# Hybrid decoder layer: prompt transposes first, two weight slots ahead of K, tile 3 ahead of the first page weights, memory tiles and last V pages one place sooner

## The reference, cut to what matters

```
h = x + W_out[ RMSNorm(stick_breaking(q, k, v)) | RMSNorm(B * conv3(C * xv)) ]     # q,k,v,B,C,xv = RMSNorm(x) @ W_in
h = h + cross_attention(RMSNorm(h), mk, mv)       # prompt: mk, mv = RMSNorm(mem) @ W_ck, @ W_cv
y = RMSNorm(h + SwiGLU(RMSNorm(h)))

def sb_block(z, mask, v, carry):
    log_om = where(mask, log_sigmoid(-z), 0)
    suffix = reverse_cumsum(log_om) - log_om + carry
    a = where(mask, exp(log_sigmoid(z) + suffix), 0)
    return a @ v, carry + sum(log_om)
```

## Time and profile before

| What | us |
|---|---|
| median of 3 runs | 1191.43 |
| their range | 1190.54 to 1193.67 |
| the profiled execution's own time | 1196.76 |
| its span (first to last instruction) | 1195.0 |
| TensorE busy in it | 1066.1 (89%) |
| VectorE, ScalarE, GpSimd busy | 665.4, 320.7, 409.5 |

### The profile page before, as it was taken

How to read it: one execution, slowest core, us unless ns; L and a number is a source line. 1 busy time by engine, 2 the same in 40 slices (tenths; PEclk the granted TensorE clock), 3 DMA queues, 4 the chain that set the end, 5 groups by cost and what they waited for, 6 DMA issues and landing times.

```text
span 1195.0 us, 28991 instructions
## 1 busy us (share of the span) xinstructions
PE 1066.1 (89%) x11527; PEld 913.7 (76%) x11527; DVE 665.4 (56%) x909; ACT 320.7 (27%) x486; POOL 409.5 (34%) x341
## 2 busy tenths in 40 slices
PE   5987999999678879787699889899999999999997
PEld 3765887866435545555599759899999999999996
DVE  2834566758478778563588348655543013544543
ACT  3511112222233524232423252412111112112121
POOL 0515354443323334344333013334333333433330
PEclk9988999999889889998799999899999999999999
DMA  9959687878999999784561132232222222231222
GB/s 352 333 167 328 203 296 245 285 268 273 392 337 329 326 325 318 277 325 146 194 227 37 40 118 91 71 106 70 82 76 72 87 94 82 72 103 44 67 66 80
DMA packets 126501, 221.16 MB, mean 185 GB/s; under 512 B 9951, under 2 KB 68580, under 8 KB 126388
## 3 DMA queue, kind: packets, MB, share of 16 engines
q1 hardware_dynamic: 103234, 146.63, 36.5%
q0 software_dynamic: 20480, 67.13, 15.9%
q10 hardware_dynamic: 2674, 5.87, 1.3%
HBM read 213.78 MB, written 5.80 MB: 184 GB/s over the span
## 4 chain that ended last, share of the span: by engine, by line
PE 66%; DVE 12%; DMA 8%; issue 5%; SPq 4%; ACT 2%; POOL 1%; POOLq 1%; DVEq 0%; ACTq 0%
PE ps L523 38%; PE ps L1664 11%; PE ps L1767 7%; DMA k_set<-in_cache_sb_k 4%; DMA mw_raw<-in_w_in 3%; DVE k_set L1342 2%; PE ps L1818 2%; SPq L618 2%; PE ps L584 2%; SPq L619 2%; DVE r_sq L699 2%; DVE r_sum L704 1%; DVE om_s L1361 1%; PE ps L367 1%; DVE h_lo L428 1%
## 5 line engine op out<-in xcount | busy, mean ns | idle before, releaser
L479 POOL TENSOR_TENSOR w_lo<-w_raw,w_hi 128x2048 fp32r<-128x2048 f32 (+3 forms) x49 | 192.9, 3939 | 404.2 <-ACT w_hi L456 363.6
L523 PE MATMUL ps<-h_hi,w_hi 128*128 128x288 f32 x832 | 180.5, 299 | 8.7 <-DVE h_lo L428 5.7
L523 PE MATMUL ps<-h_lo,w_hi 128*128 128x288 f32 x832 | 179.5, 298 | 0.0
L523 PE MATMUL ps<-h_hi,w_lo 128*128 128x288 f32 x832 | 179.5, 297 | 0.0
L1767 PE MATMUL ps<-k_set,q_blk 32*32 32x256 f32 x4096 | 135.2, 405 | 37.9 <-DVE k_set L1342 19.1
L1342 DVE STREAM_TRANSPOSE k_set<-k_set 128x1024 f32<-128x1024 f32 x128 | 149.7, 1218 | 30.2 <-DMA k_set<-in_cache_sb_k 29.5
L456 ACT ACTIVATE w_hi<-w_raw 128x2048 fp32r<-128x2048 f32 (+3 forms) x47 | 77.9, 1660 | 258.2 <-PE ps L523 228.6
L523 PEld LDWEIGHTS ps<-h_hi,w_hi 128*128 128x128 f32 x832 | 135.6, 191 | 9.7 <-issue 7.2
L1767 PEld LDWEIGHTS ps<-k_set,q_blk 32*32 32x32 f32 x4096 | 79.4, 111 | 77.7 <-issue 34.0
L970 POOL TENSOR_TENSOR mw_lo<-mw_raw,mw_hi 128x1024 fp32r<-128x1024 f32 x32 | 79.2, 2477 | 169.6 <-ACT mw_hi L1040 169.5
L523 PEld LDWEIGHTS ps<-h_lo,w_hi 128*128 128x128 f32 x832 | 135.5, 191 | 0.0
(11 more groups left out here) (266 smaller groups left out, 1684.8 us busy)
## 6 DMA issues: line engine op xcount, KB each, us to landing
k_set<-in_cache_sb_k SPq DMA_DIRECT2D x256, 256.0 KB, 4.8
v_late<-in_cache_sb_v POOLq DMA_DIRECT2D x152, 256.0 KB, 5.8
v_early<-in_cache_sb_v POOLq DMA_DIRECT2D x96, 256.0 KB, 5.1
mw_raw<-in_w_in SPq DMA_DIRECT2D x12, 1024.0 KB, 8.1
w_raw<-in_w_gate SPq DMA_DIRECT2D x11, 1024.0 KB, 5.3
w_raw<-in_w_up SPq DMA_DIRECT2D x11, 1024.0 KB, 5.3
w_raw<-in_w_down SPq DMA_DIRECT2D x8, 768.0 KB, 4.3
w_raw<-in_w_down SPq DMA_DIRECT2D x8, 640.0 KB, 4.0
```

What stands on the lines that cost most here:

```text
L479: return nc.gpsimd.tensor_tensor(w_lo[s][:, ks, :], w_raw[s][:, ks, :], w_hi[s][:, ks, :].bitcast(F32), ALU.subtract)
L523: op = nc.tensor.matmul(ps[:, 2 * t + hf, 0:b - a], weights[s][:, k, t * P:(t + 1) * P], x[:, k0 + k, a:b], start=begin and k == ks[0] and ...
```

## The change

1. TensorE: `prompt_transposes(u - 2)` comes first in a page chunk, ahead of `half_scores(C + 2, 0)`; ScalarE's copies of them come ahead of the items' copies.
2. SyncE: weight slots 2 and 3 are issued ahead of `k_half(3)` and `k_half(4)` rather than behind them.
3. TensorE: `tile(3)` stands ahead of `weight_transposes(0)`.
4. Memory tiles 24 to 31 are computed in chunks 21, 22, 23 and 25 to 29 (before 22, 23 and 25 to 30); slots 14 and 15 are loaded in iterations 23 and 26 (before 24 and 27). In chunk 21 tile 24 and the queries of the last sample pair share a place in PSUM, so `query_blocks` waits for tile 24's `evac`, and VectorE does `evac` and then `queries` ahead of all four `k_blocks`.
5. All five items of the end (mk, conv state, mv) are in chunk 30, with their copies and stores; the mv copies wait for `add_sums(29)`, and the running sums move to their last place one chunk sooner.
6. GpSimd issues V pages 248 to 255 in chunk 29 ahead of pages 244 to 247.

```
--- before.py
+++ after.py
@@ -317,7 +317,7 @@
         SPARE = (6, 2 * P)
         ITEMS = {LAST - 1: list(zip(I_K, ((5, 0), (7, 0)) * 2)), LAST: list(zip(I_V, ((5, 0), (7, 0)) * 2))}
         ITEMS.update({C: [(item, SPARE) for item in I_M[2 * i:2 * i + 2]] for i, C in enumerate((15, 17, 18, 19))})
-        ITEMS.update({CHUNKS - 2: list(zip(I_MK + I_CS, ((1, 0), (2, 0), (3, 0)))), CHUNKS - 1: list(zip(I_MV, ((1, 0), (2, 0))))})
+        ITEMS[CHUNKS - 2] = list(zip(I_MK + I_CS + I_MV, ((1, 0), (2, 0), (3, 0), (1, 0), (2, 0))))
         FIRST_ITEM = {C: sum(len(v) for k, v in ITEMS.items() if k < C) for C in range(CHUNKS + 1)}
 
         def items_of(C, part):
@@ -338,7 +338,7 @@
             _, _, kind, k = SLOTS[j // 2]
             return kind, k + j % 2
 
-        MEM_TILES = {C: TILES + i for i, C in enumerate((22, 23, 25, 26, 27, 28, 29, 30))}
+        MEM_TILES = {C: TILES + i for i, C in enumerate((21, 22, 23, 25, 26, 27, 28, 29))}
 
         def v_place(n):
             if n >= 8 * (CHUNKS - 1):
@@ -632,7 +632,7 @@
 
         def sums_at(C):
 
-            return o_sum[(C >= LAST) + (C >= 24) + (C >= CHUNKS - 2)][:, :, :]
+            return o_sum[(C >= LAST) + (C >= 24) + (C >= CHUNKS - 3)][:, :, :]
 
         def step_of(U):
 
@@ -934,12 +934,14 @@
                     sp.wait_ge(m_["rows"], LAST + 1)
                     sp.wait_ge(m_["half"], 16)
                     sp.dma_start(m_row[:, :, :], mem[0].rearrange("(m p) n -> p m n", p=P)).then_inc(s_mrow, 16)
+                if C in (1, 2):
+                    load_tiles(C + 1)
                 if C + 2 < CHUNKS:
                     k_half(sp, C + 2)
-                if 2 <= C + 1 < TILES // 2 or C + 1 in (13, 14):
+                if 3 < C + 1 < TILES // 2 or C + 1 in (13, 14):
                     load_tiles(C + 1 if C < 12 else C)
-                if C in (24, 27):
-                    load_tiles(14 + (C - 24) // 3)
+                if C in (23, 26):
+                    load_tiles(14 + (C - 23) // 3)
             sp.wait_ge(s_gt, TILES + 8)
             load_stage(sp, "out")
 
@@ -985,10 +987,14 @@
                     tile_lo(2 * C + 4)
                 if C + 1 in MEM_TILES:
                     tile_lo(MEM_TILES[C + 1])
-                v_pages(pool, range(8 * C + RING, min(8 * C + RING + 4, 8 * CHUNKS)))
+                if C == CHUNKS - 3:
+                    v_pages(pool, range(8 * CHUNKS - 8, 8 * CHUNKS))
+                if C < CHUNKS - 2:
+                    v_pages(pool, range(8 * C + RING, 8 * C + RING + 4))
                 if 2 * C + 5 < TILES:
                     tile_lo(2 * C + 5)
-                v_pages(pool, range(8 * C + RING + 4, min(8 * C + RING + 8, 8 * CHUNKS)))
+                if C < CHUNKS - 3:
+                    v_pages(pool, range(8 * C + RING + 4, 8 * C + RING + 8))
             for name in NAMES[NAMES.index("out"):]:
                 lo_stage(pool, name)
 
@@ -1043,8 +1049,8 @@
             def copy_items(C, part):
                 for n, _, (srcs, dst), (bank, c0) in items_of(C, part):
                     f = srcs[0].shape[-1]
-                    if C == CHUNKS - 1:
-                        act.wait_ge(m_["rows"], C)
+                    if n == FIRST_ITEM[CHUNKS] - MT:
+                        act.wait_ge(m_["rows"], CHUNKS - 2)
                     act.wait_ge(s_it, n + 1)
                     nc.scalar.activation(dst, tiled(ps[0:f, bank, c0:c0 + len(srcs) * P]), ACT.Copy).then_inc(s_ic, 1)
 
@@ -1121,7 +1127,7 @@
                 act.dma_start(out_k_p[0, 0].rearrange("(m p) h d -> p m (h d)", p=P), k_rows[:, :, :]).then_inc(s_kv_out, 16)
 
             def store_memory_k():
-                act.wait_ge(s_ic, FIRST_ITEM[CHUNKS - 1])
+                act.wait_ge(s_ic, FIRST_ITEM[CHUNKS - 2] + MT)
                 act.dma_start(out_mk[0, 0].rearrange("(m p) h d -> p m (h d)", p=P), mk_rows[:, :, :]).then_inc(s_out, 16)
 
             def store_memory_v():
@@ -1137,11 +1143,11 @@
                         tile_hi(2 * C + 3)
                     if 3 <= u < 19:
                         prompt_out(u - 3)
+                    if 2 <= u < 18:
+                        copy_prompt_weights(u - 2)
                     copy_items(C, 0)
                     if C == 10:
                         conv_root()
-                    if 2 <= u < 18:
-                        copy_prompt_weights(u - 2)
                     if c == 0 and g:
                         copy_new_weights(g)
                     copy_items(C, 1)
@@ -1166,8 +1172,8 @@
                         hi_parts(act, "ck", mT, G_MEM, range(KD))
                     if C == CHUNKS - 2:
                         store_memory_k()
+                        store_memory_v()
                 if last:
-                    store_memory_v()
                     act.wait_ge(s_vsum, 8 * CHUNKS - 10)
                     hi_parts(act, "out", pT[:, T_C:T_C + KC, :], None, range(KC))
 
@@ -1468,12 +1474,14 @@
                     sample_rows(g)
                 if 1 <= u < 17:
                     prompt_weights(u - 1)
-                if c == 5 and g < GROUPS - 1:
-                    queries(g + 1)
-                if more:
+                turn = c == 5 and g < GROUPS - 1
+                if more and not turn:
                     k_blocks(C + 3, range(2))
                 if C in MEM_TILES:
                     evac(MEM_TILES[C])
+                if turn:
+                    queries(g + 1)
+                    k_blocks(C + 3, range(2))
                 if more:
                     k_blocks(C + 3, range(2, 4))
                 if C == 20:
@@ -1675,8 +1683,8 @@
                             pe.wait_ge(s_gf, TILES)
                         if C == 15:
                             pe.wait_ge(s_mrow, 16)
-                    elif part:
-                        pe.wait_ge(s_ic, n - (1 if bank == 6 else 2) + 1)
+                    elif part or i >= 3:
+                        pe.wait_ge(s_ic, n + 1 - (3 if C == CHUNKS - 2 else 1 if bank == 6 else 2))
                     for j, src in enumerate(srcs):
                         f = src.shape[-1]
                         op = nc.tensor.transpose(ps[0:f, bank, c0 + j * P:c0 + (j + 1) * P], src, ident)
@@ -1841,11 +1849,11 @@
                     tile(2 * C + 2)
                 if c == 0 and g:
                     sample_rows(g)
+                if C == 0:
+                    tile(3)
                 weight_transposes(C)
                 if C == 10:
                     pe.wait_ge(s_rt["conv"], 1)
-                if C == 0:
-                    tile(3)
                 half_scores(C + 2, 0)
                 half_scores(C + 2, 1)
                 if c == 0 and g:
@@ -1863,6 +1871,8 @@
                 u, ahead = C - LAST, C + 2 < CHUNKS
                 if c % 2 == 0:
                     banks_read(C)
+                if 2 <= u < 18:
+                    prompt_transposes(u - 2)
                 if ahead:
                     half_scores(C + 2, 0)
                 items(C, 0)
@@ -1871,8 +1881,6 @@
                     tile(MEM_TILES[C])
                 if c == 0:
                     sample_rows(g)
-                if 2 <= u < 18:
-                    prompt_transposes(u - 2)
                 if c == 0:
                     new_weight_transposes(g)
                 if ahead:
@@ -1880,6 +1888,8 @@
                 items(C, 1)
                 if c == 5 and g < GROUPS - 1:
                     pe.wait_ge(m_["rows"], C)
+                    if C in MEM_TILES:
+                        pe.wait_ge(s_gf, MEM_TILES[C] + 1)
                     query_blocks(g + 1)
                 weight_transposes(C)
                 if 0 <= u < 16:
```

24 lines of the change are left out of this document (13 added, 11 removed).

## The result

| | us |
|---|---|
| after, median of 4 runs (range) | 1177.82 (1174.45 to 1182.07) |
| before, beside it, median of 4 | 1191.94 (1190.54 to 1193.67) |
| ratio, 95% interval | 0.9883 (0.9847 to 0.9918) |
| profiled execution, its span | 1178.39, 1176.6 |

1177.8 lies in the range (1161 to 1178), 0.2 us inside its upper edge; the forecast was 1166.9. The profiled executions are 18.4 us apart, the medians 14.1.

A forecast was written before the change was run, and what follows sets the result against it. TensorE's work bounds the kernel, so only its idle or half-clock stretches can give time. Opening 15.5, page stage 5.1 + 2.7 - 3.1 = 4.7 and end 4.3 sum to 24.5 us: 1191.4 to 1166.9, range 1161 to 1178.

The forecast's parts named there:

- 8.5 + 2.4: Opening: slot 3 issued sooner removes TensorE's 8.53 us gap ahead of tile 6, which then takes 6.67 instead of 9.06.
- the 4.6 for tile 3: Opening: with tile 3 first, the scores of half 2 start at 79.9 instead of 84.52, 4.6 us gained.
- Rival B: Opening: slot 3 is not what holds tile 6; 8.5 + 2.4 stay, gain 13.6 us, 1177.8; chance 0.09.
- 0.9 us to spare: Opening, ahead of tile 6: sigmoids, scan and release need 6.9 us of 7.8, so the whole gap goes.
- 5.1 + 2.7: Page chunks: 5.1 us from prompt transposes run in idle time, 2.7 from VectorE's wait for them in chunk 28.
- new waits: ... so nothing: Page chunks: moved transposes wait for the previous unit's sigmoids, holding TensorE a moment in chunk 20; cost nothing.
- Tile 24 costs 3.1: Page chunks: the memory tile moved to chunk 21 lies on the loop and costs 3.1 us; bounds 0 and 5.
- Rival A: Page chunks: transfers set the pace, transposes and VectorE give nothing, tile 24 costs 3.1; gain 16.7, 1174.7; chance 0.11.
- The end, 4.3: End of the pages: last V page lands sooner, `sample_rows` starts at 575.3 against 579.64, 4.3 us; bounds 1 and 6.
- rival C: End: gives nothing, as pages 244 to 247 are last and chunk 30 waits for them; gain 20.2, 1171.2; chance 0.06.
- From there: End: GpSimd issues pages from half 31's end at 552.97, the twelfth at 565.8 in place of 569.04.
- Landing takes 3.7 by the median: End: the last V page lands 3.7 us behind its issue, not 8.05, so 247 is there at 569.5.

The follow-up runs named there:

- e6: Before with only weight slots 2 and 3 issued ahead of K halves 3 and 4, tile 3 where it was; 1182.61 us, 0.9927 of before.
- e7: Before with only tile 3 moved ahead of the first weights' transposes, slots behind K as they were; 1188.42 us, 0.9980 of before.
- e8: After with V pages 248 to 255 on SyncE's queue behind the first two output weight slots, GpSimd issuing 244 to 247 alone; 1169.71 us, 0.9811 of before.
- e4: After with prompt transposes behind the first scores and memory tile again, ScalarE's copies in the old order; 1184.14 us, 0.9916 of before.
- e3: After with no memory tile in chunk 21, the eight tiles in chunks 22 to 29; 1174.12 us, 0.9836 of before.
- e5: After with the high and low parts of tiles 24 and 25 made in chunks 17 and 18, not 20 and 21; 1175.96 us, 0.9854 of before.
- a_again: After itself, no edit, timed and profiled once more; 1176.30 us, 0.9880 of before.
- e10: e9 with SyncE reading the eight page numbers of a K half ahead of its wait for scores; 1160.61 us, 0.9725 of before.
- e1: After with V pages 244 to 247 issued ahead of 248 to 255 again, all in chunk 29; 1172.26 us, 0.9808 of before.
- e9: After with SyncE issuing V pages 248 to 255 between the first two output weight slots, GpSimd 244 to 247 alone; 1169.32 us, 0.9801 of before.

## Why the prediction was right, and where it was off

**The sign was right, and the opening's mechanism with its size** (15.5 forecast; 14.7 to 15.6 in the traces): e6 bears out 8.5 + 2.4, and the 4.6 for tile 3 comes only with slot 2 moved too, since alone tile 3 gives 2.8 to 3.7 (e7). Rival B is out: what had "0.9 us to spare" did fit, and tile 6 has no gap. The sum said that past the opening "this arrives" whole; 0.5 to 0.8 us of it are lost again in the tile chunks, where a gap of 1.15 us ahead of tile 7 is new. The loss that the prediction worked out from the rule of the Trainium skill ("DMA: Bandwidth & Descriptors", "Queues, rings and completion order"), K behind a slot paying the slot's time, did not show as a wait in the opening: the last page of half 3 landed at 82.05 (80.66 before), and VectorE's transposes of it start at 84.99 without a wait. At the end the traces fit the rule: in e8 the pages behind two slots in SyncE's queue took 7.6 to 12.1 us, GpSimd's four among them 6.0 to 6.5.

**That the number lies in the range is partly luck.** The range's upper bound came from rival B, at 1177.8, and the measured 1177.82 meets it with B's mechanism shown to be out. Past the opening, the sum's two other terms, 4.7 and 4.3, came to 2.0 to 2.3 and 0 to 0.2 in the traces.

**Of "5.1 + 2.7" for transposes and VectorE the second part came, and the first is hardly to be seen.** VectorE's wait of 2.7 us in chunk 28 is gone in every trace with part 1, and that turn is 3.2 to 3.6 us shorter, the slower sums behind the wait included. Of the 5.1 for transposes on the chain, 1 to 1.5 us at most are left, if all of e4's 4.7 is taken, and they are within the scatter. The step that failed beside it is "new waits: ... so nothing": they come ten times, 9.2 us in all, up to 1.9 each. Whether they are what eats the 5.1 no run shows, since none takes them away. And what VectorE gained in other chunks was rightly taken as nothing.

**"Tile 24 costs 3.1" was about right in size, 2.2 by e4's one trace, and wrong in kind.** The trace of after shows 8.6 us lost from half 19's end to half 24's (the gain fell from 20.1 to 11.5) and most of it won back by half 31; e3 and e5 take tile and stall away and end 0.4 to 3.5 us from where after ends. Adding up single chunks in a stage whose turns are paced by K (half scored, eight issues in 8 us, landing in 5 to 11, VectorE) overstates both costs and gains. Rival A, that transfers set this pace, gave 16.7 in all and had 0.11. For it: the DMA engines' share is 0.81 to 0.99 in each 50 us of the stage in a_again, and in e10 half of what is saved at the issue is given back at the landing. Against it: the other half is not, and part 1 did bring its turn. So neither the forecast nor A is the whole account.

**The end, 4.3, came to nothing** (26.7 and 26.8 us): rival C, which had 0.06. Three steps of the term failed, and together they make 4.4 us. "From there": the first of the twelve pages goes out 1.3 us behind half 31, not 0.1 (1.2 us). "Landing takes 3.7 by the median": it took 6.07 (2.4 us). The sum took 8.05 for what a page costs beside the output weights and expected to escape them, "which now load 16 us sooner"; loaded sooner they run beside all twelve pages. And 6.6 us stand behind the last landing, not 5.8 (0.8 us). Behind that last step is the order: the page that lands last should have least behind it, which is what e1 restores.

So: opening 15, tile chunks -0.5 to -0.8, page chunks 2.0 to 2.3, end about 0; 16 to 17 by the two pairs of traces, 14 to 15 by the medians, against 24.5.

## To carry to other kernels

When transfers are reordered at a stage's end, cost the work behind the last landing, not the time of the last issue, and take the landing time from rows in which the same other transfers run beside; and split the last ones over queues, with what the next stage needs first ahead of them (e9, 7 us). A wait that vanishes in a loop paced by a transfer is worth what the loop's next limit leaves: measure a part by undoing it before its rows are added up. Where one trace repeats only to 2 to 4 us per stage, compare it turn by turn over all traces at hand: here one turn was 3.2 to 3.6 us shorter in all nine traces with part 1 than in all five without, while the stage's sum scattered by as much.

## What the runs showed of the hardware

VectorE stands still while GpSimd's 128x1024 subtraction runs, for some of its instructions: a copy of 64x8 took 2.32 us beside it and 0.15 alone, a 128x512 scan 3.39 and 1.22, a 128x512 add 2.68 and 0.69, and with the subtractions moved (e5) the first two were short again. Others were not held: a 128x1024 block transpose takes 1.20 us wholly beside a subtraction and alone (after, 55.4 us), `o_sum`'s add out of PSUM 0.42 and 0.42. The Trainium skill ("GPSIMD Engine Reference", section "Specifications") says that the two engines share their SBUF interfaces and contend where VectorE's instruction has two SBUF inputs or is in a 2-port mode. The scan and the 128x512 add fit it, and so do the transpose and the add out of PSUM, with one SBUF input each; for the copy no run shows the mode. How much is lost only the runs tell.

A page's landing depends on what moves beside it: in before, pages issued 1.15 us apart landed in 3.2 to 4.1 us, and the three behind the issue of 2 MB of output weights in 7.8 to 8.05.

Of the 1.09 us that SyncE needs for a page, 0.42 is the read of its number and 0.33 the issue itself; read ahead, a page takes 0.51 (349.24, 349.75, 350.26 in e10's chain).
